# Eight conditioning chunks in the first down-projection, four in the up-projection, and the ones products together at the norm behind it

## The reference, cut to what matters

```python
c_act = jax.nn.silu(c)
for layer in range(DEPTH):                       # DEPTH = 2
    mod = c_act @ ada_w[layer] + ada_b[layer]    # ada_w: 1024 x 6144 for each layer
    sh1, sc1, g1, sh2, sc2, g2 = jnp.split(mod, 6, axis=-1)
    h = rmsnorm(x, norm_g[layer, 0]) * (1.0 + sc1[:, None]) + sh1[:, None]
    y = diff_attention(h, ...) if layer == 0 else conformer_conv(h, ...)
    x = x + g1[:, None] * y
    h = rmsnorm(x, norm_g[layer, 1]) * (1.0 + sc2[:, None]) + sh2[:, None]
    x = x + g2[:, None] * conv_ffn(h, ...)       # up 1024 -> 5632, conv of 3, gate, down 2816 -> 1024
return rmsnorm(x, final_g)
```

## Time and profile before

| | |
|---|---|
| median of 3 runs | 1284.4 us (1284.37 to 1286.52) |
| the profiled execution | 1283.53 us, its span 1281.7 us |
| PE busy | 1234.9 us, 96% of the span |
| DVE busy | 695.2 us, 54% |
| ACT busy | 562.6 us, 44% |
| POOL busy | 528.6 us, 41% |
| DMA | 156.78 MB, mean 122 GB/s |
| DOWN0 | from 573 to 696 us |
| the norm behind it | from 696 to 705 us |

### The profile page before, as it was taken

How to read it: one execution, slowest core, us unless ns; L and a number is a source line. 1 busy time by engine, 2 the same in 40 slices (tenths; PEclk the granted TensorE clock), 3 DMA queues, 4 the chain that set the end, 5 groups by cost and what they waited for, 6 DMA issues and landing times.

```text
span 1281.7 us, 16893 instructions
## 1 busy us (share of the span) xinstructions
PE 1234.9 (96%) x5490; PEld 972.4 (76%) x5490; DVE 695.2 (54%) x1175; ACT 562.6 (44%) x899; POOL 528.6 (41%) x265
## 2 busy tenths in 40 slices
PE   4799999989999999999999999999999999999996
PEld 2677777767888888888888777668788888888884
DVE  4756777653676776434444999972533333331002
ACT  4356665663533444342223655663544444442221
POOL 1242333132334444344442677744244444444440
PEclk9799999999999999999999999999999999999999
DMA  9544344422355555234443222202222222232321
GB/s 344 184 145 149 121 140 153 143 99 66 131 196 181 176 183 180 99 109 156 156 166 134 68 66 72 65 27 82 77 89 96 97 90 93 96 109 95 104 87 65
DMA packets 44919, 156.78 MB, mean 122 GB/s; under 512 B 4936, under 2 KB 5192, under 8 KB 44880
## 3 DMA queue, kind: packets, MB, share of 16 engines
q1 hardware_dynamic: 43488, 153.98, 35.4%
q10 hardware_dynamic: 1392, 2.32, 0.6%
HBM read 154.15 MB, written 2.12 MB: 122 GB/s over the span
## 4 chain that ended last, share of the span: by engine, by line
PE 86%; DVE 6%; DMA 3%; issue 2%; ACT 2%; SPq 0%; DVEq 0%; ACTq 0%
PE psum L860 25%; PE psum L862 25%; PE psum L861 25%; PE psum L1126 3%; DMA ada_first<-ada_w 2%; PE psum L895 2%; PE psum L871 1%; DVE pt_lo L1342 1%; DVE psum L1333 1%; PE psum L958 1%; DVE acc L1210 1%; PE psum L907 1%; PE psum L997 0%; PE psum L888 0%; PE psum L985 0%
## 5 line engine op out<-in xcount | busy, mean ns | idle before, releaser
L462 POOL TENSOR_TENSOR w_lo<-w_raw,w_hi 128x1024 fp32r<-128x1024 f32 (+1 forms) x192 | 453.8, 2379 | 707.7 <-ACT w_hi L543 707.7
L860 PE MATMUL psum<-h_hi,w_hi 128*128 128x512 f32 x1152 | 467.1, 405 | 3.8 <-DVE x L1437 2.2
L861 PE MATMUL psum<-h_lo,w_hi 128*128 128x512 f32 x1152 | 449.9, 391 | 0.0
L862 PE MATMUL psum<-h_hi,w_lo 128*128 128x512 f32 x1152 | 449.9, 391 | 0.0
L860 PEld LDWEIGHTS psum<-h_hi,w_hi 128*128 128x128 f32 x1152 | 217.5, 189 | 55.3 <-issue 9.3
L861 PEld LDWEIGHTS psum<-h_lo,w_hi 128*128 128x128 f32 x1152 | 217.3, 189 | 46.9 <-issue 5.3
L862 PEld LDWEIGHTS psum<-h_hi,w_lo 128*128 128x128 f32 x1152 | 216.9, 188 | 46.6
L543 ACT ACTIVATE w_hi<-w_raw 128x1024 fp32r<-128x1024 f32 (+1 forms) x192 | 195.4, 1032 | 73.4 <-DMA w_raw<-w_tiles 73.4
L860 PE MATMUL psum<-a_hi,w_hi 128*128 128x512 f32 x352 | 137.4, 390 | 0.8 <-issue 0.8
L862 PE MATMUL psum<-a_hi,w_lo 128*128 128x512 f32 x352 | 137.0, 389 | 0.0
L861 PE MATMUL psum<-a_lo,w_hi 128*128 128x512 f32 x352 | 137.0, 389 | 0.0
(11 more groups left out here) (184 smaller groups left out, 1361.6 us busy)
## 6 DMA issues: line engine op xcount, KB each, us to landing
w_raw<-w_tiles SPq DMA_DIRECT2D x160, 512.0 KB, 3.3
ada_buf<-ada_w SPq DMA_DIRECT2D x32, 512.0 KB, 3.4
ada_mid<-ada_w SPq DMA_DIRECT2D x32, 512.0 KB, 4.5
w_raw<-w_tiles SPq DMA_DIRECT2D x32, 448.0 KB, 3.1
ada_first<-ada_w SPq DMA_DIRECT2D x16, 512.0 KB, 6.2
ada_late<-ada_w SPq DMA_DIRECT2D x16, 512.0 KB, 4.6
x<-x_in SPq DMA_DIRECT2D x4, 512.0 KB, 10.9
bias<-rel_scratch ACTq DMA_DIRECT2D x1, 2048.0 KB, 8.2
```

Of the source, the lines that this page charges most:

```text
L462: nc.gpsimd.tensor_tensor(w_lo[:, slot, 0:k], w_raw[:, (ph.tile + l) % 2, 0:k], f(w_hi[:, slot, 0:k]), ALU.subtract).then_inc(lo_done, 1)
L860: nc.tensor.matmul(dst, w_hi[:, slot, k], rhs_hi, start=first, stop=False)
L861: nc.tensor.matmul(dst, w_hi[:, slot, k], rhs_lo, start=False, stop=False)
L862: return nc.tensor.matmul(dst, w_lo[:, slot, k], rhs_hi, start=False, stop=last)
```

## The change

MID goes from 8 to 4, a constant LATE = 8 is new, and `acc_late` gets eight sums instead of one (they fill the place of `h_lo`). Chunks 12 to 15 stay in UP0. Chunks 16 to 23 are worked in DOWN0, two a body: DVE takes the four pieces of one ahead of `residual(i, 0)` and the four of the other ahead of `residual(i, 1)`. The eight ones products of these chunks run at the norm, one ahead of `square_sum` and seven behind it, where the 18 dummy products of `keep_warm` stood. They write 32 columns of PSUM bank 3. The writes of `h_lo` wait for the products, since the sums lie there. The 32 columns of `mod` are made in one DVE operation behind the norm, and PE waits for it ahead of the second pair of PW1, which writes bank 3. The gated bias of PW2 is made there too.

```diff
-MID = 8
+MID = 4
+LATE = 8
-        acc_late = at("acc_late", [P, S], F32, h_base + 4 * 2 * S * 4)
+        acc_late = at("acc_late", [P, LATE, S], F32, h_base + 4 * 2 * S * 4)
...
-            def load_late(i, n):
-                sp.wait_ge(ada_used, lin(i, 2 * (4 * LATE_CH + n - 3), 8))
-                sp.dma_start(ada_late[:, n].rearrange("p k n -> p (k n)"), piece(ada_w, lin(i, 4 * LATE_CH + n, 4)))\
-                  .then_inc(ada_late_landed[n], 16)
+            def load_late(i, q):
+                sp.wait_ge(ada_used, lin(i, 2 * (4 * LATE_CH + q - 3), 16))
+                sp.dma_start(ada_late[:, q % 4].rearrange("p k n -> p (k n)"), piece(ada_w, lin(i, 4 * LATE_CH + q, 8)))\
+                  .then_inc(ada_late_landed[q % 4], 16)
...
                 for l in range(6):
                     load_tile(DOWN0, i, l)
-                    if l < 4:
-                        load_late(i - 1, l)
+                    for q in ((0, 1), (2, 3), (), (4, 5), (6, 7), ())[l]:
+                        load_late(i - 1, q)
             for l in range(4):
                 load_tile(PW1, 0, l)
-                load_late(DOWN0.bodies - 1, l)
+                for q in (2 * l, 2 * l + 1):
+                    load_late(DOWN0.bodies - 1, q)
...
                     group(i, c)
-                    if c == 0:
-                        late_ada(acc_late, LATE_CH, i - 1)
-            late_ada(acc_late, LATE_CH, DOWN0.bodies - 1)
+            def last_ada(q):
+                pe.wait_ge(ada_used, 8 * (LATE_CH + q + 1))
+                ada_product(WARM, acc_late[:, q], at_=4 * q)
+            last_ada(0)
             square_sum(2, 1)
-            keep_warm(18)
+            for q in range(1, LATE):
+                last_ada(q)
...
+                if t == 1:
+                    pe.wait_ge(sc_read, LATE0 + MID + 1)
...
                     if m > lo:
+                        if n == 2:
+                            dve.wait_ge(ada_mm, LATE_CH + m)
                         dve.wait_ge(h_hi_ready, HI_AT[n] + m)
...
-            def down0(i, first):
-                residual(i, 0, DOWN0, DK, 1, GATE[1])
-                if not first:
-                    late_out(LATE_CH, i - 1)
-                for n in range(4):
-                    dve.wait_ge(ada_late_landed[n], lin(i, 16, 16))
-                    ada_piece(ada_late[:, n], acc_late, n, lin(i, 8 * LATE_CH, 8))
-                residual(i, 1, DOWN0, DK, 1, GATE[1], last=isinstance(i, int) and i == DOWN0.bodies - 1)
+            def late_pieces(i, c):
+                for q in range(4 * c, 4 * c + 4):
+                    dve.wait_ge(ada_late_landed[q % 4], lin(i, 16 * (c + 1), 32))
+                    for kk in range(2):
+                        k = 2 * (q % 4) + kk
+                        ada_part(ada_late[:, q % 4, kk], k, tile_of(acc_late, lin(i, c, 2)),
+                                 lin(i, 8 * (LATE_CH + c) + k, 16))
+            def down0(i):
+                for c in range(2):
+                    late_pieces(i, c)
+                    residual(i, c, DOWN0, DK, 1, GATE[1], last=isinstance(i, int) and i == DOWN0.bodies - 1 and c == 1)
...
-            late_out(LATE_CH, DOWN0.bodies - 1)
+            norm(2)
+            late_out()
             V.tensor_tensor(gated_bias[:], mod[:, GATE[2]:GATE[2] + DK],
                             prm[:, PARAMS["b_pw2"]:PARAMS["b_pw2"] + DK], ALU.mult).then_inc(dve_step, own.tick())
-            norm(2)
+            dve.wait_ge(dve_step, own.now())
```

31 lines of the change are left out of this document (18 added, 13 removed).

## The result

The changed kernel takes 1335.61 us in the median (1333.36 to 1339.05) against 1285.38 us (1284.37 to 1286.52) for the kernel before on the same chip: 1.0398 times as long (the two medians alone give 1.0391), with a 95% interval of 1.0380 to 1.0416. The forecast was 1318.5 us with a range of 1302 to 1327. The sign and the kind of loss were right, the size was too small. The profiled execution of after took 1333.36 us; its span is 1331.6 us, 49.9 more than the 1281.7 us before. What follows is reckoned in spans. R stands for the start of a residual, R7 for the start of the last one.

The account below looks back on a forecast made before the run. The prediction took PE, busy 96% of the span, to bound the kernel by its own order. Against the profiled 1283.53 us, -3.8 (UP0) + 30.7 (DOWN0) + 8.1 (norm) = +35.0 gave 1318.5 us, range 1302 to 1327.

Parts of the forecast that it names:

- What bounds the kernel: Whole kernel: PE is busy 96% of the span, so its own order is on the path.
- the loop: DOWN0: a residual starts weight splits, these let SP issue the last pieces, the next residual waits for them; 19.6 us.
- Part 1: UP0: four ones products leave PE's path at 0.95 us each, 3.8 us saved ahead of DOWN0.
- Part 2: DOWN0: twice the pieces, each chunk ahead of its residual, make a loop of waits; DOWN0 grows by 30.7 us.
- The issue of the last piece: DOWN0: SP issues a chunk's last piece behind the weight tiles, at R + 12.75.
- Its landing: DOWN0: six transfers, 3.08 MB from R + 7.73, take 7.6 us plus 2.8 fixed; last piece there at R + 18.1.
- DVE's work behind it: DOWN0: the last piece's two operations take 1.54 us, then the next residual starts at R + 19.6.
- Part 3: Norm: ones products and the start of PW1 run at a low clock; costs 8.1 us, ends at -0.6 and +9.
- (a): Rival, DOWN0: pieces land in time, PE sets the pace, all seven products gained; -7.3 us, 1276.2 us; chance 0.07.
- (b): Rival, DOWN0: residuals only 17.3 to 18.5 us apart, less idle time ahead of the norm; 1290 to 1309 us; chance 0.10.
- (c): Rival, DOWN0: the clock stays low, five or six groups add 9 us each; about 1365 us; chance 0.05, or longer.
- (d): Rival, DOWN0: chunk worked behind the residual, which the change doesn't move; ruled out by DVE's order; 0.02 near no change.

Follow-up runs that it names:

- the first experiment: Changed kernel with two lines swapped: in DOWN0 DVE works each residual first and the chunk of pieces behind it; 1281.98 us against 1284.80 for the kernel before.
- experiment 56: Not a separate run: the text reads "the first experiment", then "56 passes"; changed kernel with DOWN0's residual ahead of the pieces, 1281.98 us against 1284.80.
- part 1 alone: Kernel before with MID = 4 and chunks 20 to 23 left out, DOWN0 and the norm as they were; 1281.13 us against 1284.68, ratio 0.9973.

## Why the prediction was right and wrong

**What bounds the kernel: right.** PE's order set the pace before; with the loop opened it does so again (all eight residuals of the first experiment wait for PE).

**Part 1: right.** Forecast -3.8 us; measured -3.8 in the changed kernel, -3.75 with the residual first, -4.0 with part 1 alone. The further 2.9 us in DOWN0 that the forecast gave only if PE set the pace appeared in the first experiment, 2.9 us, and were lost in the loop otherwise.

**Part 2: the mechanism was right, the size was off.** The loop stood in the trace of before without having cost anything there, and every one of its stations is in the trace of after: R + 1.49 for the splits, R + 11.4 for the last low part, PE waiting for POOL ahead of six groups, residuals without a bracket. The miss is the term "the next residual starts at R + 19.6". It is 21.4, and six of these rounds are 10.7 of the 12 us by which DOWN0 was undersized; the first residual came 1.8 us later than forecast by the same term, the last round was 0.5 us shorter. On average over the six rounds the terms came out like this:

- *The issue of the last piece* was right: forecast R + 12.75, measured R + 12.5 to R + 13.1, 12.8 on average.
- *Its landing* was forecast at R + 18.1 and came at R + 18.7 to R + 20.0, 19.3 on average. The step that failed is "the queue moves 410 GB/s when it is full; with 405 ... 7.6 us".
- *DVE's work behind it*, "its two operations take 1.54 us", took 2.0 us. When the last piece landed DVE was still busy with the third, which had landed only 0.6 to 1.3 us earlier. That is why four operations in 3.1 us stand behind DVE's last wait (it ends at R + 18.3 on average), and why halving the second operations took 1.41 us off the round.

So 1.2 of the 1.8 us are the transfers and 0.5 the operations. The sum treated the six transfers as one stream of 3.08 MB. In the round from 592.91 they are two bursts (stretches of half a microsecond and one of 10.5, columns as above):

```profile
606.00:606.50 0.50, 0.50 (x4) 0.41 (x3) 0.46 (x2) 0.00 (x0) 0.00 (x0) 1.00 0.52 75
...
607.00:607.50 0.50, 0.50 (x4) 0.41 (x3) 0.50 (x1) 0.00 (x0) 0.00 (x0) 1.00 0.95 301
...
601.00:611.50 10.50, 8.66 (x38) 6.85 (x37) 2.74 (x4) 0.95 (x1) 2.07 (x1) 1.00 0.88 293
```

From 601.0 to 606.0 as much had moved as the first three transfers hold (1.6 MB), and the queue ran almost dry before the last three (1.51 MB, issued from 604.46 on) got going. These took until 611.5, near 290 GB/s from 606.5 on, where 1.51 MB had 3.7 us in the prediction's own bound from the second issue. The rate of 410 itself was no freak of half a microsecond: in the trace of before the half microseconds from 656.5 to 661 show 385 to 426 GB/s but for one of 254, and at the end of the changed kernel's DOWN0 the mean was 415 from 730 to 735. What failed is to carry it over to this burst. Why the burst is slower, at a DMA share of 0.95 in the row shown, isn't settled.

The Trainium skill ("DMA: Bandwidth & Descriptors", Specifications) has 358 GB/s as the limit of HBM for one core; by it, as an estimate, the six transfers take 8.6 us. That is nearer to the 10.5 us of the trace than 7.6, but it isn't the reason: 415 GB/s over 5 us stand above that figure in the same trace, and the mean of 293 well below it.

**Part 3: the size was right, the cause half wrong.** Forecast R7 + 15.2 and 1.7 us for a cold start; measured R7 + 15.13 and 2.0. Ten idle microseconds did make the clock low, as the text had it. But the text also had it that at full clock the seven chunks would take 7 x 0.81 = 5.7 us and gain 0.6. In no run did they: in the first experiment, without any gap, the clock fell to 1.2 GHz 3.2 us into the ones products, and with 24 dummies in the gap it fell as they began. Without the loop the norm cost 2.5 us and the rest 2.3 more, so the lower end of part 3, -0.6, was 5.4 us too low for the change as it is written. The forecast also took all 11.9 us as cold, while its own reading of the earlier trace rows gave full clock back within 4 to 6 us of steady work. That this came right is luck: the prediction had no reason why ones products don't bring the clock back, and part of the steady work in the earlier trace rows was ones products.

**Two figures of the working.** The tile and the piece whose landing took 5.4 us are 0.52 MB each, 1.05 MB and 2.6 us instead of 0.98 MB and 2.4; that leaves the 2.8 us that was taken, so nothing hangs on it. Three weight tiles and four pieces are 3.54 MB in a group, not 3.4.

**The rivals.** (a) *The pieces land in time*: the point from which it decides (a loop under 15.2 us) was right, and its time of 1276.2 too low, for the most part by the cold norm; the two kernels in which only the loop is opened took 1282.0 and 1282.2. (b) *The loop at its lower bound*: none of the six rounds was that short, and even half the bytes gave 18.9. (c) *The clock in DOWN0*: the long waits did make groups start at 1.2 GHz. Three groups of after, behind 1.84, 6.51 and 4.77 idle us:

```profile
604.00:609.00 5.00, 4.66 (x20) 3.86 (x21) 2.74 (x4) 0.00 (x0) 0.29 (x1) 1.00 0.92 276
626.00:631.00 5.00, 4.85 (x11) 3.81 (x12) 2.74 (x4) 0.00 (x0) 0.10 (x1) 0.50 0.87 298
...
669.00:674.00 5.00, 4.62 (x11) 3.70 (x12) 2.74 (x4) 0.00 (x0) 0.33 (x1) 0.50 0.89 296
```

The Trainium skill ("TensorE: Matmul & The Clock Gate", HAM oscillation) tells of tiles that each start cold behind a wait; the groups behind 4.77 and 6.51 us agree. But nothing became longer by it: the group at 626.15 ends some 2.5 us later than at full clock, and the weights of the next are there only at 647.7, so the loop hides it. As the bound of the stage (c) fell. (d) *The residual isn't moved*: it was, as the DVE timeline shows. The first experiment is the kernel that (d) speaks of.

## What to carry to other kernels

Before work is put ahead of an instruction that others wait for, follow what frees the buffers of its own loads: here a chunk, 11.5 us of DVE in the first experiment, fitted into a group of 14.9, but its last pieces were queued behind weight tiles that only the residual set free, and one swap of two lines, or the same loads issued one group earlier, was worth 53 us. Size transfers that are issued in two bursts burst by burst, and give the rate a range: on one queue 1.5 MB moved at 290 GB/s here and 2 MB at 415. Ask of each piece, not only of the last, whether the engine that works it will be free. Small matmuls put together in one place may cost more than spread out: behind such a row TensorE's granted clock was at 1.2 GHz here although PE had been busy. Read the granted clock, not only whether PE is busy.

## What the runs showed of the hardware

**The clock can fall while PE is busy.** In the first experiment 56 passes of 128x128 by 128x1 ran without a gap, behind full clock, and the clock went to 1.2 GHz 3.2 us into them (at 694.7). Behind 24 dummies and the little work of `square_sum` it went as they began, and it stayed down for all 11.92 us of them. In the first experiment it came back at 704.9, 4.6 us behind the first matmul of PW1. With four chunks and three dummies of 128 columns behind each of the first three it stayed up, in two runs; with seven chunks and two dummies behind each it fell; with four chunks and no dummies it fell in the idle time behind them. Fourteen passes behind 28 dummy passes were followed by 3.4 us at 1.2 GHz. What decides isn't settled by these runs.

**DVE beside POOL.** The eight operations of a chunk take 11.5 us where POOL makes low parts in between, and near 6.2 us where it is idle. Both are from the first experiment, ahead in DOWN0 and at the norm:

```profile
587.21 11.02 DVE L1219 SCALAR_TENSOR_TENSOR acc_late<-ada_late,cact,acc_late 128x512 f32 x7
...
690.21 5.67 DVE L1219 SCALAR_TENSOR_TENSOR acc_late<-ada_late,cact,acc_late 128x512 f32<-128x512 f32 x7
```

That is 1.57 against 0.81 us for one on average. It isn't spread evenly: of the first seven the median takes 0.75 us and the longest 2.82. POOL worked 7.3 us within the first stretch (587.08 to 596.11 with a gap of 1.7) and not at all in the second. The Trainium skill ("GPSIMD Engine Reference", Specifications) says that GpSimd's interfaces to SBUF are shared with VectorE, with contention for VectorE instructions that have two SBUF inputs, as these have. The trace agrees, with a factor near two over the whole. In the changed kernel it didn't show (the longest of the 56 took 0.75 us), because the operations there waited for their pieces until POOL was done.
